# Expert blocks of a two-layer decoder: which operand of the first products stays in TensorE, and in which order blocks and weight loads follow

## The reference, cut to what matters

```
def hier_moe(x, w_rg, b_rg, w_re, b_re, w1, w3, w2):
    ...  # top-1 of 4 groups, then top-2 of its 4 experts: gates (b, t, 16)
    h = jax.nn.silu(jnp.einsum('btd,edf->btef', x, w1)) * jnp.einsum('btd,edf->btef', x, w3)
    return jnp.einsum('btef,efd->btd', h * gates[..., None].astype(x.dtype), w2)
```

## Time and profile before

| | us |
|---|---|
| median of three runs | 1856.72 |
| lowest and highest | 1854.28, 1858.73 |
| the profiled execution | 1842.92 |
| its span, first to last instruction | 1841.0 |
| busy in the span: PE, PEld | 1510.5, 1003.0 |
| busy in the span: DVE, ACT, POOL | 628.0, 365.6, 186.0 |

### The profile page before, as it was taken

How to read it: one execution, slowest core, us unless ns; L and a number is a source line. 1 busy time by engine, 2 the same in 40 slices (tenths; PEclk the granted TensorE clock), 3 DMA queues, 4 the chain that set the end, 5 groups by cost and what they waited for, 6 DMA issues and landing times. The chain is left out here.

```text
span 1841.0 us, 22772 instructions
## 1 busy us (share of the span) xinstructions
PE 1510.5 (82%) x9044; PEld 1003.0 (54%) x9044; DVE 628.0 (34%) x1344; ACT 365.6 (20%) x705; POOL 186.0 (10%) x138
## 2 busy tenths in 40 slices
PE   6999988788798299995199999786897947999960
PEld 3455455555545288884144655554564436888840
DVE  1141245646644200002402314466464450000015
ACT  1000023323201022221510001332230011222214
POOL 0001001010000500002600010010100013000026
PEclk9999998879889599998599999988887968999985
DMA  7229244456232488886231304444724046888952
GB/s 275 58 68 317 77 129 153 145 123 143 76 110 101 173 316 339 339 351 256 80 98 46 119 6 122 132 154 135 138 104 140 0 195 225 343 338 339 362 197 82
DMA packets 135909, 317.68 MB, mean 173 GB/s; under 512 B 51348, under 2 KB 81556, under 8 KB 114708
## 3 DMA queue, kind: packets, MB, share of 16 engines
q1 hardware_dynamic: 106640, 187.44, 28.9%
q0 software_dynamic: 12672, 86.51, 15.3%
q10 hardware_dynamic: 16516, 42.63, 6.1%
HBM read 267.35 MB, written 49.19 MB: 172 GB/s over the span
## 5 line engine op out<-in xcount | busy, mean ns | idle before, releaser
L1603 PE MATMUL ps<-ring,xT 128*128 128x512 f32 (+1 forms) x896 | 365.2, 568 | 1.3 <-ACT xT L749 1.3
L1930 PEld LDWEIGHTS ps<-z,ring 128*128 128x128 f32 x2432 | 295.3, 198 | 19.2 <-issue 17.0
L1930 PE MATMUL ps<-z,ring 128*128 128x128 f32 x2432 | 295.6, 283 | 1.4 <-ACT z L749 1.4
L1603 PEld LDWEIGHTS ps<-ring,xT 128*128 128x128 f32 x896 | 169.6, 191 | 186.4 <-issue 181.5
L749 ACT ACTIVATE ring<-ps 128x512 f32<-128x512 f32 (+2 forms) x186 | 95.9, 539 | 376.4 <-PE ps L1704 189.2
L749 ACT ACTIVATE z<-ps 128x512 f32<-128x512 f32 (+1 forms) x152 | 78.8, 543 | 411.5 <-PE ps L1930 222.0
L996 DVE TENSOR_TENSOR z<-ps,vbuf 128x512 f32<-128x512 f32 (+3 forms) x84 | 47.6, 570 | 327.8 <-PE ps L1603 295.0
L1940 PE MATMUL ps<-ring,z 128*128 128x512 f32 x304 | 140.4, 605 | 6.3 <-DVE z L996 2.0
L996 DVE TENSOR_TENSOR z<-z,ps 128x256 f32<-128x256 f32 x38 | 16.0, 421 | 322.5 <-ACT z L749 322.5
L1885 PE MATMUL ps<-ring,xT 128*128 128x512 f32 x256 | 114.6, 608 | 2.4 <-DMA ring<-in_w_out 1.9
L1704 PE MATMUL ps<-tab,kbuf 128*128 128x128 f32 x512 | 92.4, 310 | 12.9 <-DMA kbuf<-in_cache_k,idx_k 7.6
(11 more groups left out here) (246 smaller groups left out, 1652.6 us busy)
## 6 DMA issues: line engine op xcount, KB each, us to landing
ring<-in_w SPq DMA_DIRECT2D x114, 1024.0 KB, 7.2
ring<-in_w_in SPq DMA_DIRECT2D x12, 2048.0 KB, 8.5
z<-expert_rows ACTq DMA_DIRECT2D x38, 512.0 KB, 5.1
expert_rows<-z ACTq DMA_DIRECT2D x38, 512.0 KB, 4.4
expert_rows<-zero SPq DMA_DIRECT2D x1, 12288.0 KB, 53.4
ring<-in_w_out SPq DMA_DIRECT2D x4, 2048.0 KB, 10.9
vbuf<-in_b_in SPq DMA_DIRECT2D x2, 1670.0 KB, 10.6
ring<-in_w_in SPq DMA_DIRECT2D x2, 1072.0 KB, 5.7
```

Source lines behind the costliest of these rows:

```text
L1603: m = mm(ps[0:n, i % 4, 0:w], xTv[:, k, t * P:t * P + n], slab[at % 3][:, k, 0:w], start=(k == 0), stop=(k == KD - 1))
L1930: m = mm(ps[:, 2 + s, at:at + BLOCK], w13[s][:, w, q, c::2], xgT[s][:, q, :], start=(q == 0), stop=(q == KD - 1))
```

## The change

First products. The transposed tokens `xgT` are now stationary and the weights move: `[128, 2, 256]` of w1 and w3 at once, 512 columns, so 8 products instead of 32. h comes out with tokens on the partitions. Silu and the product are done there (in place in `sil`), then TensorE transposes the result in two pieces (`pe_turn_h`) into the same PSUM bank, and VectorE copies it to `hT` (`dve_turn`). `h_ps` and `hT_sb` count twice a block.

Order. On TensorE: first products of k, token transposes of k+1, output products of k-1, h transposes of k, first products of k+1. ScalarE and VectorE follow the same order: `act_gate` of k before `act_out` of k-1; on VectorE the product of k, the copy of the output of k-1, the copy of transposed h of k. The first block and the last pair stand outside the loops, so `plan`'s last value is one lower and each engine adds one.

Weight loads. SyncE issues w1 and w3 of block k+2 after the first products of k, then w2 of k+1 after the output products of k-1, block by block.

More of the change, by code:

```diff
@@ L944, in turn_block, with act_gate @@
                             f(xgT[s][:, 4 * hf:4 * hf + 4, :], ps[:, hf, :].rearrange("p (k n) -> p k n", k=4), ACT.Copy).then_inc(xgT_sb, 1)
-                    def act_block(i, k, s, more, turn):
+                    def act_gate(k, s, more, turn):
                         if more:
                             load_block(k + 2, s)
-                        act.wait_ge(h_ps, k + 1)
+                        act.wait_ge(h_ps, k * 2 + 1)
                         f(sil[s], ps[:, 2 + s, 0:2 * BLOCK], ACT.Silu).then_inc(sil_sb, 1)
@@ L952, in act_block, with act_out @@
                             turn_block(k * 2 + 2, 1 - s)
+                    def act_out(stored_, k, s):
                         act.wait_ge(y_ps, k + 1)
-                        act.wait_ge(y_out[s], i * 16 + 16)
+                        act.wait_ge(y_out[s], stored_)
                         f(yo[s][:, SLAB:], ps[:, 5 + 2 * s, :], ACT.Copy).then_inc(y_sb, 1)
@@ L963, in _ @@
                     turn_block(0, 0)
-                    with act.Fori(0, last_pair) as i:
-                        act_block(i, i * 2, 0, True, True)
-                        act_block(i, i * 2 + 1, 1, True, True)
-                    lp = last_pair
-                    act_block(lp, lp * 2, 0, False, True)
-                    act_block(lp, lp * 2 + 1, 1, False, False)
+                    act_gate(0, 0, True, True)
[4 more added lines that the diff above has]
+                        act_out(i * 16, i * 2 - 1, 1)
+                    lp = last_pair
+                    act_gate(lp * 2 - 1, 1, True, True)
+                    act_out(lp * 16, lp * 2 - 2, 0)
+                    act_gate(lp * 2, 0, False, True)
+                    act_out(lp * 16, lp * 2 - 1, 1)
+                    act_gate(lp * 2 + 1, 1, False, False)
+                    act_out(lp * 16 + 16, lp * 2, 0)
+                    act_out(lp * 16 + 16, lp * 2 + 1, 1)
                     for s in range(2):
@@ L1481, in _, with dve_out @@
                     link(V.tensor_reduce(r_plan[:, N_BLOCKS:], r_even, AX.X, ALU.add))
-                    link(V.tensor_scalar(r_plan[:, N_BLOCKS:], r_plan[:, N_BLOCKS:], float(EXPERTS // 2 - 1), None, ALU.add))
+                    link(V.tensor_scalar(r_plan[:, N_BLOCKS:], r_plan[:, N_BLOCKS:], float(EXPERTS // 2 - 2), None, ALU.add))
                     V.tensor_copy(plan[:, :], r_plan[0:1, :]).then_inc(planned, 1)
                     dve.wait_ge(planned, 2)
-                    last_pair = dve.value_load(plan[0:1, N_BLOCKS:N_BLOCKS + 1], min_val=EXPERTS // 2 - 1, max_val=N_BLOCKS // 2 - 1)
-                    def dve_block(k, i, s):
+                    last_pair = dve.value_load(plan[0:1, N_BLOCKS:N_BLOCKS + 1], min_val=EXPERTS // 2 - 2, max_val=N_BLOCKS // 2 - 2) + 1
+                    def dve_gate(k, s):
                         dve.wait_ge(sil_sb, k + 1)
-                        tt(hT[s].rearrange("p a n -> p (a n)"), sil[s], ps[:, 2 + s, 2 * BLOCK:], ALU.mult).then_inc(hT_sb, 1)
+                        tt(sil[s], sil[s], ps[:, 2 + s, 2 * BLOCK:], ALU.mult).then_inc(hT_sb, 1)
+                    def dve_turn(k, s):
+                        dve.wait_ge(h_ps, k * 2 + 2)
+                        V.tensor_copy(hT[s].rearrange("p a n -> p (a n)"), ps[:, 2 + s, 0:2 * BLOCK]).then_inc(hT_sb, 1)
+                    def dve_out(k, i, s):
                         dve.wait_ge(y_ps, k + 1)
@@ L1495, in _ @@
                     dve.sem_inc(y_sb, 3)
-                    with dve.Fori(0, last_pair + 1) as i:
-                        dve_block(i * 2, i, 0)
-                        dve_block(i * 2 + 1, i, 1)
+                    dve_gate(0, 0)
+                    dve_turn(0, 0)
+                    with dve.Fori(1, last_pair + 1) as i:
+                        dve_gate(i * 2 - 1, 1)
+                        dve_out(i * 2 - 2, i - 1, 0)
+                        dve_turn(i * 2 - 1, 1)
+                        dve_gate(i * 2, 0)
+                        dve_out(i * 2 - 1, i - 1, 1)
+                        dve_turn(i * 2, 0)
+                    lp = last_pair
+                    dve_gate(lp * 2 + 1, 1)
+                    dve_out(lp * 2, lp, 0)
+                    dve_turn(lp * 2 + 1, 1)
+                    dve_out(lp * 2 + 1, lp, 1)
                     for t in tiles:
@@ L1911, in _ @@
                     pe.wait_ge(planned, 2)
-                    last_pair = pe.value_load(plan[0:1, N_BLOCKS:N_BLOCKS + 1], min_val=EXPERTS // 2 - 1, max_val=N_BLOCKS // 2 - 1)
+                    last_pair = pe.value_load(plan[0:1, N_BLOCKS:N_BLOCKS + 1], min_val=EXPERTS // 2 - 2, max_val=N_BLOCKS // 2 - 2) + 1
                     def pe_turn(i, s):
@@ L1935, in pe_y @@
                         pe.wait_ge((w2_in0, w2_in1)[s], i * 16 + 16)
-                        pe.wait_ge(hT_sb, k + 1)
-                        pe.wait_ge(y_sb, k * 2 + 1)
+                        pe.wait_ge(hT_sb, k * 2 + 2)
+                        pe.wait_ge(y_sb, k * 2 + 3)
                         for hf in range(2):
```

9 lines of the change are left out of this document (6 added, 3 removed).

## The result

The changed kernel takes 1823.72 us in the median of six runs (1817.96 to 1833.7) against 1855.5 for the kernel before (six runs, 1849.31 to 1860.34). The ratio is 0.9835 with a 95% interval of 0.9801 to 0.9868: 24 to 37 us faster. Forecast were 22.2 us, 1834.5, with a range down to 1827. The direction was right and the gain was larger than the range allowed.

What follows compares the result with a forecast made beforehand. TensorE was taken to bound the expert blocks: 6.96 + 0.88 + 3.53 + 0.22 = 11.59 us a block against 12.23. With stage ends, 11.7 and 10.5 us saved, 22.2 in all, giving 1834.5 us; range 1827 to 1848.

Steps and rivals of the forecast that it cites:

- token transposes: TensorE's eight transposes of tokens in each block, forecast at 0.88 us.
- h transposes: Two added TensorE transposes of h in each block, forecast at 0.22 us with no gap around them.
- gap after block 0: At stage start, block 1's first products wait for ScalarE's copies: 1.77 us after block 0's end.
- last output products: At stage end, they start 5.03 us after the start of the output products before them.
- block 0 of layer one: First products partly at the low clock, surplus of 1.44 us kept: 8.40 us.
- Block 0 of layer two: First products partly at the low clock, surplus of 1.81 us kept: 8.77 us.
- The 0.53 isn't a result of the wait: TensorE's first record of a 512-column group takes 0.53 us even without waiting, the others 0.429.
- rival B: The 0.10 us of each 512-column group goes: 7.2 us more saved, saving 29, 1827.4 us; chance 0.06.
- Rival A: TensorE loses 0.3 us a block to split moving operand or 0.26 to bubbles at short transposes; chance 0.14.
- Cost nothing: New weight-load order: loads land in time, and a block's bytes need 10.2 us at 411 GB/s, inside the period.
- Rival C: Stage turns transfer-bound at TensorE's wait for first weights, below 343 GB/s; 1860 to 1882 us; chance 0.07.
- ScalarE's table load: 1.28 us once a pair at the loop head, idle time behind it; costed at nothing, 0.6 a block if uncovered.

Runs made afterwards that it cites:

- e0_after: The changed kernel run again without edits; median 1821.25 us, ratio 0.9828 to the kernel before.
- e4_cols20: Changed kernel plus two unused products of 20 columns (four records) ahead of each block's first products; stages 213.7 and 236.3 us, period 11.86 us.
- e5_cols128: Changed kernel plus two unused products of 128 columns (four records) ahead of each block's first products; stages 213.4 and 235.8 us.
- e1_order: Kernel before with only output products one block later and the new order of weight loads; median 1844.78 us, ratio 0.9945.
- e9_after: The changed kernel run again without edits, on one chip with another version; median 1825.26 us, ratio 0.9848 to the kernel before.
- e3_loads: Changed kernel with the old order of weight loads; median 1880.35 us, ratio 1.0148 to the kernel before.
- e8_reads: Changed kernel with the old order of weight loads, next pair's experts read before the wait for output products; median 1854.9 us, ratio 0.9999 to the kernel before.
- e6_extra: Changed kernel with 1 MiB more loaded for each block from the third on (w2 a second time); a pair takes 24.98 us, one run.
- e2_form: Kernel before with only the new form of first products, old block order and old weight loads; median 1880.78 us, ratio 1.0144.

## Why the prediction was wrong

The mechanism was right: the stage stays bound by TensorE, no transfer or other engine stands in the chain, and most of its terms are off by 0.05 us or less (token transposes 0.89 for 0.88, h transposes 0.23 for 0.22, gap after block 0 1.77 and 1.78 for 1.77, last output products 4.99 and 4.98 after the ones before for 5.03, block 0 of layer one 8.39 for 8.40). Block 0 of layer two took 8.37 for 8.77; since e0_after had 10.02 there, it is luck that this term came so near.

The step that failed is "The 0.53 isn't a result of the wait". I charged 0.10 us to each 512-column group, 6.96 and 3.53 instead of 6.87 and 3.44, so 11.59 instead of 11.41 a block. 34 full steps x 0.18 = 6.1 us, which with the 0.4 of block 0 is the difference between 28.6 and 22.2. The period of 11.41 was rival B, which I gave 0.06 because of the earlier trace rows. The reading of those rows was wrong: I took the longer first step and did not see that the 16 short records ahead of it had gained time. A group's cost must be read with its neighbours, from a point where TensorE's weight load is as far ahead as at the other end (e4_cols20 and e5_cols128 show it). In e1_order the output products alone show that the wait was the cause.

The estimate for the median then was 1855.5 - 28.6 = 1826.9, just past the end of the range. The remaining 3 us to 1823.72 are not explained by a trace; e0_after and e9_after, at 1821.25 and 1825.26, put them within what medians of six runs vary.

Rival A (split moving operand, bubbles at the short groups): no sign of either; 0.43 for each record in two runs of 256 columns, as in contiguous ones.

"Cost nothing" for the weight loads was right for the kernel as changed, and left out what the reader needed most. I compared slack and landing time in the new order only. The landing of w3 itself went from 7.0 to 8.5 us (median) in the changed kernel, well inside the 16.2. The old order would have had 11.9 us for it, and by e3_loads and e8_reads it would have taken back all of the gain and more: reads of the plan stand in the late queue (2.2 us), and landings grow to 10.7 and 11.9 when the requests come bunched. Rival C's threshold, an average of 343 GB/s, was the wrong quantity: e8_reads stalls at 328 on the average, with the engines at 421 in e6_extra, since TensorE waits for one load and not for the average.

ScalarE's table load, which I kept and took to be covered, is gone from the loop: the kernel before has one at the head of each loop pass, the changed one has none between 1539.9 and 1773.4. It was and is off TensorE's path.

The parts don't add. The order on TensorE and the new loads alone give 11.9 us in the stages, the form alone costs 12.2, form and block order with the old loads cost 23.6 (3.6 with the reads moved), and all three together give 28.6.

## What to carry to other kernels

Where TensorE sets the pace, a product that follows a met wait has its weight load begun ahead of it, and one that waits pays 0.10 us for it on top: count both when a wait goes. When compute gets shorter, check each load's issue point, with what stands ahead of it in its queue and with what else is asked for in those microseconds; the mean bandwidth doesn't tell. And in a kernel whose other stretches vary by 20 us, read a change from its stage in the trace, and use the median for the sign.

## What the runs showed of the hardware

- The busy share of the DMA engines isn't the share of their bandwidth: the changed kernel shows 0.99 at 364 GB/s with no load late, e6_extra 1.02 at 421.
- Transfers held 421 GB/s over 160 us on one core (e6_extra), nine tenths of it loads and one tenth stores.
- The first 0.12 us of a weight load lie ahead of the product when TensorE isn't made to wait (1647.94 and 1648.06 in the changed kernel). Four records of 20 columns gain 0.08 us over four of 128, and the group of 512-column records behind them takes 0.08 longer, at no cost in sum (e4_cols20, e5_cols128).
- In e3_loads TensorE idled 1.9 to 2.1 us for a weight transfer in each pair, and behind 10 of the 15 stalls the granted clock fell (16 records took 8.82 us instead of 7.13). In e8_reads it idled 1.4 to 1.9 us, and the clock fell behind 2 of 15, both of 1.9 us.
- The same instructions of the mixing block ran at a mean granted clock of 0.87 in one execution (63.4 us, e0_after) and 0.66 in another (84.2 us, e2_form).
